# Modulation sums moved to VectorE, rotation tables in groups, a broadcast spread out, two accumulators exchanged

## The reference, cut to what matters

```python
# first block
h = x + 0.5 * swiglu(rmsnorm(x, g1), w_gate, w_up, w_down)          # "ffn1", d_ff 5504
q, k, v, u = split(rmsnorm(h, g) @ w_in)                             # "w_u", "w_qkv"
y_ssm = s5_mixer(u, ...)                                             # complex diagonal scan, gelu, "glu"
y_att = dilated_attention(q, k, v)                                   # first attention, 16 heads
h = h + concat(rmsnorm(y_ssm), rmsnorm(y_att)) @ w_out               # "w_out"
h = h + 0.5 * swiglu(rmsnorm(h, g2), ...)                            # "ffn2"
# second block
shift, scale, gate   = split(silu(c) @ w_mod + b_mod, 3)             # modulation, w_mod 2048 x 6144
shift_c, scale_c, _  = split(silu(c_ctx) @ w_mod + b_mod, 3)
u   = layer_norm(x) * (1 + scale) + shift
u_c = layer_norm(ctx) * (1 + scale_c) + shift_c
... mLSTM branch a, attention branch b, both gated ("x_...", "ba", "bb")
out = layer_norm(ALPHA * x + gate * (merged @ w_out_2))              # "wo"
```

## Time and profile before

| | us |
|---|---|
| median of 3 runs | 3326.79 |
| lowest, highest | 3325.24, 3328.04 |
| profiled execution, its own time | 3327.47 |
| its span | 3325.7 |

### The profile page before, as it was taken

The page is one execution under the profiler, slowest core; times in us unless marked ns, Lnnn a source line. Parts: engine busy times, 40 slices in busy tenths (PEclk is TensorE's granted clock), DMA queues, the critical chain, the costliest instruction groups (busy, mean ns, idle before and its releaser), DMA issues.

```text
span 3325.7 us, 43272 instructions
## 1 busy us (share of the span) xinstructions
PE 3256.4 (98%) x16088; PEld 2637.7 (79%) x16088; DVE 1851.5 (56%) x2157; ACT 1507.9 (45%) x1867; POOL 423.2 (13%) x641
## 2 busy tenths in 40 slices
PE   8999999999998999999999999999999999989998
PEld 6777778888776877788888888888878877877886
DVE  5444445455896554445556564556665754444556
ACT  4444444444335543444444434544455555534443
POOL 1111113944762001000000000000000100010000
PEclk9999999999999999999999999999999999999999
DMA  7777776556543467766665556546866643675654
GB/s 237 255 251 251 253 249 201 188 189 194 149 133 105 165 187 250 226 189 189 175 208 197 204 184 184 171 146 179 163 151 185 189 128 97 177 176 160 210 181 152
DMA packets 308182, 621.72 MB, mean 187 GB/s; under 512 B 19848, under 2 KB 28304, under 8 KB 307392
## 3 DMA queue, kind: packets, MB, share of 16 engines
q1 hardware_dynamic: 290480, 555.91, 53.7%
q0 software_dynamic: 17552, 63.79, 7.9%
HBM read 614.37 MB, written 2.10 MB: 185 GB/s over the span
## 4 chain that ended last, share of the span: by engine, by line
PE 93%; DVE 4%; ACT 1%; DMA 1%; POOL 1%; issue 1%; SPq 0%; ACTq 0%; DVEq 0%; POOLq 0%
PE acc L277 23%; PE acc L278 23%; PE acc L279 23%; PE pst L966 2%; PE acc L966 2%; PE acc L967 2%; PE pst L967 2%; PE pst L968 2%; PE acc L968 2%; DVE w_lo L245 2%; PE pst L700 1%; PE pst L2650 1%; DMA w_raw<-in_w_in 1%; PE pst L2632 1%; PE pst L2342 1%
## 5 line engine op out<-in xcount | busy, mean ns | idle before, releaser
L245 DVE TENSOR_TENSOR w_lo<-w_raw,w_hi 128x1024 fp32r<-128x1024 f32 x1060 | 1333.6, 1263 | 1270.8 <-ACT w_hi L238 1267.7
L238 ACT ACTIVATE w_hi<-w_raw 128x1024 fp32r<-128x1024 f32 x1060 | 1121.0, 1060 | 1538.6 <-PE acc L279 1209.0
L277 PE MATMUL acc<-w_hi,act_hi 128*128 128x512 f32 (+1 forms) x3360 | 1335.3, 397 | 25.9 <-DVE w_lo L245 20.5
L278 PE MATMUL acc<-w_lo,act_hi 128*128 128x512 f32 (+1 forms) x3360 | 1307.8, 389 | 0.0
L279 PE MATMUL acc<-w_hi,act_lo 128*128 128x512 f32 (+1 forms) x3360 | 1307.5, 389 | 0.0
L277 PEld LDWEIGHTS acc<-w_hi,act_hi 128*128 128x128 f32 x3360 | 633.9, 189 | 177.8 <-issue 42.3
L279 PEld LDWEIGHTS acc<-w_hi,act_lo 128*128 128x128 f32 x3360 | 633.8, 189 | 131.6
L278 PEld LDWEIGHTS acc<-w_lo,act_hi 128*128 128x128 f32 x3360 | 634.5, 189 | 121.5 <-issue 0.5
L687 POOL DMA_DIRECT2D mod_ring<-in_w_mod x96 | 69.3, 724 | 704.2 <-PE pst L700 531.1
L966 PE MATMUL pst<-w_hi,g_hi 128*128 128x512 f32 x344 | 136.7, 397 | 0.0
L966 PE MATMUL acc<-w_hi,g_hi 128*128 128x512 f32 x344 | 136.5, 397 | 0.0
(11 more groups left out here) (455 smaller groups left out, 2394.4 us busy)
## 6 DMA issues: line engine op xcount, KB each, us to landing
w_raw<-in_w_in SPq DMA_DIRECT2D x400, 512.0 KB, 3.7
w_raw<-in_ffn_w_down SPq DMA_DIRECT2D x168, 512.0 KB, 3.7
w_raw<-in_ffn_w_gate SPq DMA_DIRECT2D x160, 512.0 KB, 3.9
w_raw<-in_ffn_w_up SPq DMA_DIRECT2D x160, 512.0 KB, 4.4
mod_ring<-in_w_mod POOLq DMA_DIRECT2D x96, 512.0 KB, 6.0
w_raw<-in_w_out SPq DMA_DIRECT2D x64, 512.0 KB, 4.0
w_raw<-in_w_branch_a SPq DMA_DIRECT2D x32, 512.0 KB, 4.1
w_raw<-in_w_branch_b SPq DMA_DIRECT2D x32, 512.0 KB, 4.5
```

The lines of the kernel that those rows point to most:

```text
L238: act.activation(weight_tiles(s)[0], w_raw[:, s % SLOTS, :], ACT.Copy).then_inc(w_hi_done, 1)
L245: dve.tensor_tensor(lo, w_raw[:, s % SLOTS, :], hi.bitcast(F32), ALU.subtract).then_inc(w_lo_done, 1)
L277: pe.matmul(o, xh, wh, start=k == 0, stop=False)
L278: pe.matmul(o, xh, wl, start=False, stop=False)
```

## The change

It has these parts, all in one diff:

1. The modulation is summed on VectorE. A pass is one block of 512 columns for one of the two vectors: 16 operations of 128 x 512 (`w * c + part`, the partial sum in PSUM), each waiting for the one before. Then TensorE sums over the partitions with four matmuls of one column (`mod_sum_pe`), and VectorE adds the bias. There are 20 passes and 160 loads, since c and c_ctx are no longer taken together: 9 passes in ffn1 (blocks 1 to 9), 10 in ffn2 (blocks 1 to 10), 1 in the first quarter of the down product of ffn2. VectorE, not TensorE, waits for silu of c. `mod_scale_dve` moves from ahead of the first down product to ahead of the second.
2. Table levels w = 1 to 16 are formed in scratch memory in the last quarter of ffn1's down product. When w_u starts they are copied, and the levels 32 and 64 are formed in four groups of eight tiles, each reported by itself. The scan steps wait for their group; `SSM_SKIP` is 5, the tail 4.
3. The gate row is turned and copied ahead of x_zb, and its 16 broadcasts are issued one for every two chunks of x_zb.
4. glu takes `acc[:, 1]`, the first attention `acc[:, 0]`; w_out starts on `acc[:, 0]` and ends on `acc[:, 1]`.
5. The turns of `ha` are called two chunks sooner on ScalarE and VectorE (24 and 25 in place of 26 and 27).

```diff
-        def mod_chunk_pe(pe, n_use, blk, n):
...
-                for hc in range(2):
-                    j, at_ = 32 * (2 * kk + hc), (2 * kk + hc) * SEQ
-                    mm = pe.matmul(pst[j:j + 32, 2, 0:SEQ], c, mod_ring[n_use][n % 2][:, at_:at_ + SEQ],
-                                   start=n == 0, stop=n == 7)
-            mm.then_inc(mod_used, 1)
...
+        def mod_loads_pool(pool, first, last):
+            for n in range(first, last):
                 if n >= 2:
-                    pool.wait_ge(mod_used, n - 1)
...
+                    pool.wait_ge(mod_used, 2 * n - 2)
+                pool.dma_start(mod_ring[int(n >= 8 * MOD_PASSES["ffn2"])][n % 2][:].rearrange("p (k n) -> p k n", k=2),
+                               cols(A["w_mod_2"], 2 * (n % 8), MOD_BLOCK[n // 8] * BLK)).then_inc(mod_ready[n % 2], 16)
+        def mod_pair_dve(dve, n_use, mod, n):
+            p, _, v = mod
+            dve.wait_ge(mod_ready[n % 2], p * 64 + 16 * (n // 2 + 1))
+            part = pst[:, 2, :]
+            for k in (2 * n, 2 * n + 1):
+                w, c = mod_ring[n_use][n % 2][:, (k % 2) * BLK:(k % 2 + 1) * BLK], c_act[:, k, v:v + 1]
+                if k == 0:
+                    ins = dve.tensor_scalar(part, w, c, None, ALU.mult)
+                else:
+                    dve.wait_ge(mod_used, p * 16 + k)
+                    ins = dve.scalar_tensor_tensor(out=mod_sum[:] if k == KT - 1 else part, in0=w, scalar=c, in1=part,
+                                                   op0=ALU.mult, op1=ALU.add)
+                ins.then_inc(mod_used, 1)
+        def mod_sum_pe(pe, p):
+            pe.wait_ge(mod_used, p * 16 + 16)
+            pe.wait_ge(mod_added, p + 1)
+            for t in range(4):
+                mm = pe.matmul(pst[:, 3, t:t + 1], mod_sum[:, t * P:(t + 1) * P], ones_col[:], start=True, stop=True)
+            mm.then_inc(mod_summed, 1)
...
+                    for j in range(16):
+                        split_ahead(dve, s, 16, i, 16, j + LEAD, j + LEAD + 1)
+                        if j == 7:
+                            lo_tiles(dve, n_use, b - 1)
+                        if mod is not None and j % 2 == 0:
+                            mod_pair_dve(dve, n_use, mod, j // 2)
...
+        def near_tables_pool(pool, steps):
+            pool.wait_ge(w_used, AT["ffn1"][0] + 16 * NB + 3 * DOWN_CHUNKS + 6)
...
+            while w < SCRATCH:
+                table_level_pool(pool, steps, near_cos, near_sin, near_tmp, slice(0, ST), w)
                 w *= 2
+        def ssm_tables_pool(pool, steps):
+            for o, i in ((rot_cos, near_cos), (rot_sin, near_sin)):
+                steps.did(pool.tensor_copy(o[:, :, 0:SCRATCH], i[:]))
+            steps.settle()
+            for g in range(4):
+                tiles = slice(g * TABLE_TILES, (g + 1) * TABLE_TILES)
+                for w in (SCRATCH, 2 * SCRATCH):
+                    table_level_pool(pool, steps, rot_cos, rot_sin, turn_tmp, tiles, w)
+                pool.sem_inc(tables_ready, 1)
-        SSM_SKIP = 8
+        SSM_SKIP, SSM_TAIL = 5, 4
...
-                            o = acc[:, 0, h, :]
+                            o = acc[:, 1, h, :]
...
             for k in range(KT):
+                pool.wait_ge(w_used, AT["x_zb"][0] + 2 * k + 1)
                 pool.dma_start(gate_row[:, k * P:(k + 1) * P],
...
-            stream_split(act, "x_gb", sg_fetch(act, sg_b), ha_ahead(turn_act, act, 26))
+            stream_split(act, "x_gb", sg_fetch(act, sg_b), ha_ahead(turn_act, act, 24))
...
+            gate_rows_dve(dve)
             stream_split(dve, "x_zb", gated_dve(dve, ob, 8))
-            gate_rows_dve(dve)
-            stream_split(dve, "x_gb", between=ha_ahead(turn_dve, dve, 27))
+            stream_split(dve, "x_gb", between=ha_ahead(turn_dve, dve, 25))
```

More of the change, by code:

```diff
@@ L199, in build @@
         mod_ready = [sem("mod_ready0"), sem("mod_ready1")]
-        mod_used, mod_copied, mod_picked, mod_added, mod_done = (
-            sem("mod_" + n) for n in ("used", "copied", "picked", "added", "done"))
+        mod_used, mod_summed, mod_added, mod_done = (sem("mod_" + n) for n in ("used", "summed", "added", "done"))
         cx_loaded, cx_ready, cx_turned, cx_hi, cx_lo = (
@@ L664, in build, with mod_pass @@
         LAST = D_FF - (NB - 1) * BLK
[L666 to L667 removed]
+        MOD_PASSES = {"ffn1": 0, "ffn2": 9}
+        MOD_BLOCK = tuple(range(8)) + (8,) + tuple(range(8)) + (9, 10, 11)
+        N_MODS = len(MOD_BLOCK)
+        def mod_pass(n_use, b):
+            if isinstance(b, int):
+                p = b - 1 + 9 * n_use
+                return p, MOD_BLOCK[p], 0
+            return b + (9 * n_use - 1), b - 1, 1 - n_use
@@ L704, in mod_copy_act @@
[L704 to L715, removed]
@@ L827, in it @@
                 ins.then_inc(fetched[1], 1)
-                if blk is not None:
-                    mod_add_dve(dve, blk)
+                if mod is not None:
+                    mod_add_dve(dve, mod)
             ffn_iterations(dve, name, it)
         def ffn_pe(pe, name, n_use, turning):
[L834 to L844, removed]
+            def it(b, s, c, p, i, mod):
+                block_product(pe, s, c, act_hi, act_lo, 0, 8, p, None, turning if first(b) else None, n=width(b),
                               first_k=ROW_SLOT[2 * n_use])
@@ L847, in it @@
                     turn_gated(pe, n_use, b - 1, p - 1)
[L848 to L852, removed]
+                block_product(pe, s + 8, c + 8, act_hi, act_lo, 1, 8, p, None, n=width(b), first_k=ROW_SLOT[2 * n_use])
+                if mod is not None:
+                    mod_sum_pe(pe, mod[0])
             ffn_iterations(pe, name, it)
         TURN_AT = 4
+        MOD_LAST_AT = tuple(range(LEAD, LEAD + 16, 2))
         down_banks = (acc[:, 0, :, :], pst[:, 2:4, :], acc[:, 1, :, :], pst[:, 0:2, :])
@@ L947, in down_pe @@
                             rows_turn_pe(pe, 1, p)
+                    if not chained and q == 0 and j == DOWN_CHUNKS - 3:
+                        mod_sum_pe(pe, N_MODS - 1)
                     if q == 1 and j == 0:
-                        pe.wait_ge(mod_added, 13 if n_use else 10)
+                        pe.wait_ge(mod_added, N_MODS + 1 if n_use else MOD_PASSES["ffn2"] + 1)
                     if not chained and j in CX_TURN_AT[q]:
@@ L1520, in tt @@
                 steps.did(pool.tensor_tensor(o, a, b, op))
-            steps.did(pool.tensor_copy(rot_cos[:, :, 0:1], pr(COS2).unsqueeze(2)))
-            steps.did(pool.tensor_copy(rot_sin[:, :, 0:1], pr(SIN2).unsqueeze(2)))
+            shape = [P, tiles.stop - tiles.start, w]
+            ec, es = (x[:, tiles, w - 1:w].broadcast_to(shape) for x in (cos, sin))
+            co, si = cos[:, tiles, 0:w], sin[:, tiles, 0:w]
+            nc_, ns_ = cos[:, tiles, w:2 * w], sin[:, tiles, w:2 * w]
+            t = tmp[:, tiles, 0:w]
@@ new lines, in table_level_pool @@
+            tt(nc_, co, ec, M)
+            tt(ns_, co, es, M)
+            tt(t, si, es, M)
+            steps.settle()
+            tt(nc_, nc_, t, S)
+            steps.settle()
+            tt(t, si, ec, M)
+            steps.settle()
+            tt(ns_, ns_, t, A_)
+            steps.settle()
+        def near_tables_pool(pool, steps):
+            pool.wait_ge(w_used, AT["ffn1"][0] + 16 * NB + 3 * DOWN_CHUNKS + 6)
+            steps.did(pool.tensor_copy(near_cos[:, :, 0:1], pr(COS2).unsqueeze(2)))
+            steps.did(pool.tensor_copy(near_sin[:, :, 0:1], pr(SIN2).unsqueeze(2)))
```

154 lines of the change are left out of this document (67 added, 87 removed).

## The result

The changed kernel takes 3281.51 us in the median of four runs (3278.69 to 3285.41), the kernel before, on the same chips, 3326.22 (3325.24 to 3328.04). The ratio is 0.9865, with a 95% interval from 0.9853 to 0.9877. The forecast was 3240, so half of the expected 87 us did not come. The profiled execution took 3282.46 us by its own time, 3280.4 by its span; against the 3327.47 of before that is -45.0.

What follows compares the result with a forecast made beforehand. TensorE, busy 98%, bounds the kernel, so only its work and standstills count. Terms -50.2 (modulation), -1.7 (silu of c), -8.1, -12.9, -5.1, -8.7 (parts 2 to 5) sum to -86.7: from 3327.47 to 3240, range 3228 to 3262.

Steps and rivals of the forecast that it cites:

- It hides in VectorE's wait for ScalarE: ffn blocks: VectorE's added 16 operations per pass, 11.8 us, fit its idle time; 75% busy in 45.3 us.
- a w_lo is made about 5 us ahead of its use: ffn blocks: VectorE makes w_lo about 5 us early, so a slip of a few us costs nothing.
- Removed and added on TensorE: Modulation on TensorE: 66.8 us removed over 12 blocks, 16.6 added by sums of 20 passes (0.83 each); net -50.2.
- Gate row: x_gb: spacing the 16 broadcasts removes TensorE's 11.4 us wait and its clock loss; -12.9, bounds -8 to -12.9.
- Tables: After 800 us: shorter table operations remove two w_lo waits with their clock loss; -8.1, bounds 0 and -8.1.
- Accumulators and the turns of ha: At ffn2's start the w_out read-out wait goes, -5.1; turning ha two chunks sooner removes its waits, -8.7.
- The wait for the last scan output: Scan steps: TensorE's wait of 2.0 us at the last output stays, outputs being four chunks apart.
- the -86.7 of the sum: Whole kernel: all forecast terms added together, -86.7 us, taken from the profiled execution's 3327.47.
- The ring: Rival, modulation blocks: w_mod loads landing in over 8.6 us set the pace; 3450 at 12 us landing; 4%.
- The stretching: w_mod loads: VectorE holding GpSimd's shared port would lengthen landing; forecast kept its sum, citing an exemption for the new operations.
- The scan steps: Rival: scan steps start three chunks sooner and run into unfinished tables, GpSimd 8 us later than forecast; 3256; 13%.
- 3277 by side waits that come back: Rival, TensorE: only its work goes, -50.2, while waits return elsewhere (w_lo, broadcasts, ha turns); 3277; 8%.

Runs made afterwards that it cites:

- last pair later: Changed kernel with only the eighth, last pair of each modulation pass one chunk later on VectorE; 3349.34 us, ratio 1.0068.
- sooner pair: Changed kernel with the last seven of the eight pairs of each modulation pass one chunk sooner on VectorE; 3234.16 us, ratio 0.9729.
- part 1 alone: Kernel before with only the modulation part; tables, gate row, accumulators and turns of ha left as before; 3314.72 us, ratio 0.9965.

## Why the prediction was right or wrong

**The step that failed** is "It hides in VectorE's wait for ScalarE". As to VectorE's throughput it was right: an operation 0.75 us (0.74 forecast), busy time +209 (some 230 forecast), no wait of TensorE for w_lo in either ffn. But I followed only what stands behind a pair on VectorE, the next w_lo, and not the last pair's own reader. The forecast says "a w_lo is made about 5 us ahead of its use"; the sum has no such lead. It is wanted the moment TensorE ends chunk 15, the last, and its last pair can begin only some 2.4 us after chunk 14 is used, behind hi and lo. hi, lo and the pair are 1.06 + 1.23 + 1.5 = 3.8 us (4.0 in the rows above) against the 2.72 of chunk 15, all of them numbers that the forecast used, so this could have been worked out before the run. Its cost, which the forecast put at nothing: 25.9 us of waits. That the last pair's place is the cause is shown by moving it both ways: later by itself, 3349 us, and sooner together with the six before it, 3234.

**The clock behind short waits.** I charged 1.5 us to waits of over 2 us and nothing to shorter ones. Here waits of 1.14 to 1.3 us cost 1.6 us too, behind 11 of 18, and those of about 4 us do behind all 19 (last pair later). The clock therefore took nearly as much as the waits: 27.2 us lost after, where 5.1 are left without them.

**The terms that stood.** Removed and added on TensorE: 45.38 - 44.44 = 0.94 us for a pass instead of 0.83, +2 us over 20. (The 0.5 and 1.23 that bounded this term stand in no row, gives 0.36 and 1.09 for the same things; the 0.94 lies between either pair.) Blocks with the sooner pair 45.38 where 45.3 was forecast. Gate row 13.4 (12.9). Tables 5.6 by medians, some 2 by ratios, 6.7 by waits (8.1; within its bounds). Accumulators and the turns of ha were not run by themselves; what is left of the side parts' 33.2 for them is 33.2 - 13.4 - 5.6 = 14.2 (13.8), or some 3 more with the tables at 2. The wait for the last scan output stayed at 2.0, as said. With the last pair in time the kernel gains 91.9 us by medians, of which 9.3 are the next term; the other 82.6 stand against the -86.7 of the sum.

**A term that was not there.** The shift of g_hi and g_lo: 176 chunks x 0.053 = -9.3 us. It was luck, and it hid part of the miss. Waits, clock, sums, tables and shift together: -86.7 + 25.9 + 22.1 + 2.2 + 2.5 - 9.3 = -43.3, where -45.0 was measured; the tables' term alone is known to no better than 3 us, so the last us of this agreement say nothing.

**The rivals.** The ring did not pace: a chunk of w_mod lands 5.0 us after its issue in the median, not later than in the earlier trace rows, and VectorE waits for one once, 1.2 us. VectorE did 320 operations of 0.75 us beside these loads, which now went out singly and not in twos. The stretching that the Trainium skill ("SBUF — State Buffer", "SBUF: two separate sides") describes did not show, which agrees with the exception in "Who interferes with whom". The scan steps did not run into the tables: GpSimd finished them at 836. The rival that gives nearly the time measured, 3277 by side waits that come back, is wrong all the same: the side waits went, as "part 1 alone" shows, and part 1 gave 11 us, the shift included, instead of 52. The time alone would have confirmed it.

## What to carry to other kernels

When work moves to a less loaded engine, follow its last piece to its reader: what is that piece queued behind, when can that start, and when does the busy engine want the result. A share of 63% says nothing of it; here one pair placed a chunk sooner or later made 3234 or 3349 us out of 3282. And when small tiles are added or dropped, look whether a large operand has moved in SBUF, and compare the pitch of its matmuls: a gain or loss of that kind is easily credited to whatever else was changed.

## What the hardware showed

- A stationary operand's place in SBUF changes the pitch of 128x128 by 128x512 matmuls at full clock: with g_hi and g_lo at 0, 64 or 96 bytes beyond a multiple of 128, twelve matmuls of the down products take 2.721, 2.747 or 2.800 us (0.227, 0.229, 0.233 each), in three, seven and two kernels. In the bb product this order did not hold: 2.80 with both halves on a multiple of 128, 2.77 in the changed kernel.
- A wait of 1.14 to 1.3 us within otherwise dense matmuls lowered TensorE's clock to 1.2 GHz for some 3 us behind 11 of 18 of them, the one wait of 0.6 us (sooner pair) did not, and waits of about 4 us did in 19 of 19 (last pair later). Each of these waits runs into the 0.9 us of one-column matmuls of the sum; those alone lowered nothing in the wide blocks, not even made twice (blocks of 45.38 and 46.27 us at full clock), while a wait of 1.0 us ahead of a doubled sum did. No experiment parts the wait from them. What sets the 11 apart from the 7 was not tried.
